# Feed-forward of a float32 block chain on one core: next group's operands made later in a step, early tiles evicted unscaled, sums of the first activations put off to the down product

## What is computed

```python
D_FF = int(math.ceil(8 * D_MODEL / 3 / 256)) * 256      # 2816

def _swiglu(xn, w_gate, w_up, w_down):
    g = jnp.einsum('bsd,df->bsf', xn, w_gate)
    up = jnp.einsum('bsd,df->bsf', xn, w_up)
    return jnp.einsum('bsf,fd->bsd', jax.nn.silu(g) * up, w_down)

        h = _swiglu(_rmsnorm(x, pre_ffn_g[layer]), ffn_w_gate[layer], ffn_w_up[layer], ffn_w_down[layer])
        x = x + _rmsnorm(h, post_ffn_g[layer])
```

## Time and profile before

| what | value |
|---|---|
| median of 3 runs | 4546.69 us (4539.64 to 4556.09) |
| the profiled execution | 4558.02 us |
| its span (first to last instruction) | 4555.0 us |
| PE busy | 4088.6 us (90% of the span) |
| DVE busy | 2750.5 us (60%) |
| ACT, POOL busy | 1402.6 us (31%), 1232.8 us (27%) |
| mean granted TensorE clock | 0.933 of full |
| the two feed-forwards | near 530 to 1220 us and near 1960 to 2650 us |

### The profile page before, as it was taken

One profiled execution on the slowest core, in us unless ns is written; L12 is line 12 of the kernel. 1 busy time (PEld: TensorE's weight loads), 2 busy tenths in 40 slices (PEclk: granted clock), 3 DMA queues, 4 the chain that ended last, 5 costly groups with the idle time before them and its releaser, 6 DMA issues.

```text
span 4555.0 us, 48262 instructions
## 1 busy us (share of the span) xinstructions
PE 4088.6 (90%) x18826; PEld 3185.6 (70%) x18826; DVE 2750.5 (60%) x3035; ACT 1402.6 (31%) x1771; POOL 1232.8 (27%) x586
## 2 busy tenths in 40 slices
PE   7899799989889998889998868998999999899778
PEld 6457677877666666768776657886888888766556
DVE  6744788887754543488887766214665664365543
ACT  4333322233332333232233332222222222155311
POOL 1002144444312322134444421221211111121141
PEclk9999899999899999999999988998999998899788
DMA  2002223343310001222234332222111112221242
GB/s 101 19 14 77 75 97 104 102 140 125 114 56 19 24 19 33 93 81 98 98 120 146 111 116 74 99 96 99 36 56 59 52 59 92 75 94 54 81 145 86
DMA packets 124811, 368.43 MB, mean 81 GB/s; under 512 B 12708, under 2 KB 13352, under 8 KB 118568
## 3 DMA queue, kind: packets, MB, share of 16 engines
q1 hardware_dynamic: 124584, 365.36, 23.4%
HBM read 268.31 MB, written 96.99 MB: 80 GB/s over the span
## 4 chain that ended last, share of the span: by engine, by line
PE 62%; DVE 28%; ACT 3%; DMA 3%; issue 2%; POOL 1%; SPq 0%; DVEq 0%; POOLq 0%; ACTq 0%
PE ps L355 21%; PE ps L1261 13%; PE ps L426 7%; PE ps L772 2%; PE ps L2656 2%; PE ps L2668 2%; DVE h L1430 2%; PE ps L1980 2%; PE ps L2664 2%; PE ps L1972 1%; DVE xop L1421 1%; DVE ua L1560 1%; DVE h L1441 1%; DMA f<-h_keep 1%; PE ps L3706 1%
## 5 line engine op out<-in xcount | busy, mean ns | idle before, releaser
L308 POOL TENSOR_TENSOR wlo<-wraw,whi 128x1024 fp32r<-128x1024 f32 x177 | 429.5, 2427 | 1899.1 <-ACT whi L300 1794.7
L1261 PE MATMUL ps<-xop,whi 128*128 128x512 f32 x1984 | 618.8, 393 | 8.4 <-DVE xop L1421 4.0
L1261 PE MATMUL ps<-top,whi 128*128 128x512 f32 x1488 | 491.2, 413 | 93.3 <-DVE vb L1521 49.3
L300 ACT ACTIVATE whi<-wraw 128x1024 fp32r<-128x1024 f32 x177 | 187.5, 1059 | 1067.0 <-PE ps L355 729.4
L1261 PEld LDWEIGHTS ps<-xop,whi 128*128 128x128 f32 x1984 | 372.8, 188 | 94.9 <-DVE xop L1421 4.8
L1261 PEld LDWEIGHTS ps<-top,whi 128*128 128x128 f32 x1488 | 291.6, 198 | 175.5 <-DVE vb L1521 52.7
L1261 PE MATMUL ps<-xop,wlo 128*128 128x512 f32 x992 | 389.0, 392 | 0.0
L426 PE MATMUL ps<-xhalf,whi 128*128 128x512 f32 x1024 | 378.1, 452 | 5.2 <-POOL wlo L308 5.2
L1610 POOL TENSOR_TENSOR wlo<-wsum,whi 128x1024 fp32r<-128x1024 f32 (+2 forms) x108 | 248.1, 2298 | 470.9 <-ACT whi L1286 470.0
L355 PE MATMUL ps<-xhi,whi 128*128 128x512 f32 x912 | 328.8, 443 | 39.8 <-DVE xlo L561 25.9
L355 PE MATMUL ps<-xhalf,whi 128*128 128x512 f32 x1024 | 280.8, 397 | 27.4 <-DVE xhalf L561 14.4
(11 more groups left out here) (571 smaller groups left out, 7714.0 us busy)
## 6 DMA issues: line engine op xcount, KB each, us to landing
wraw<-in_w_dram SPq DMA_DIRECT2D x177, 512.0 KB, 3.7
h_keep<-h SPq DMA_DIRECT2D x154, 256.0 KB, 4.3
wraw<-in_s_dram SPq DMA_DIRECT2D x48, 512.0 KB, 4.2
f<-h_keep SPq DMA_DIRECT2D x24, 768.0 KB, 5.3
wmore<-in_s_dram SPq DMA_DIRECT2D x32, 512.0 KB, 4.1
x_keep<-x SPq DMA_DIRECT2D x16, 1024.0 KB, 3.9
g_keep<-gates SPq DMA_DIRECT2D x64, 256.0 KB, 2.4
gb<-g_keep SPq DMA_DIRECT2D x32, 512.0 KB, 5.3
```

The lines of the kernel that those rows point to most:

```text
L300: se.own().activation(K.hi(c), K.raw[:, c % NRAW, :], ACT.Copy).then_inc(*K.S(("hi", c)))
L308: ge.own().tensor_tensor(K.lo(c), K.raw[:, c % NRAW, :], K.hi(c).bitcast(F32), SUB).then_inc(*K.G(("lo", c)))
L1261: d = pe.e.matmul(out[:, s, :], w[:, o], x[:, i, :], start=(j < 3 and i == 0 and t == 0), stop=(i == k - 1 and t == 2), skip_group_check=True)
```

## The change

It does five things in each feed-forward.

1. In the lead all four tiles of pair 0 are evicted by ACT as they are (`evict(i, m)`), so the up tiles leave PSUM by ACT and not by DVE's product. DVE scales all four in SBUF after the first operand, and multiplies gate by up later (`early_product`, unit 2 of step 0).
2. The four sums of pair 0 are no longer made in step 0. Its four products are stored as halves (`early_store`), loaded back in unit 3 of step 10 (`early_load`), summed on DVE at the end of step 10, and the sums stored at the beginning of step 11.
3. Pair 0 takes the last place in `h_keep` (`ORDER`), with the weight rows packed to match, so that its sums are needed by the last set only.
4. A set's operands are made later: high parts at j - 3, low parts at j - 4. So ACT makes operands 0 to 3 in the last step of a set and 4 to 6 in the first of the next, DVE 0 to 2 and 3 to 6. Of those, operand 5 and 6 now come after U2 on DVE.
5. ACT's operand 5 of step 0 waits for the four early stores in place of seven stores.

The diff, without the two lines that only rename:

```diff
+ORDER = [*range(1, 11), 0]
...
-        self.early = [at(eb + o * KB, [128, 1024], F32, "h") for o in (-16, -12)]
-        h = self.early
-        self.hq0 = [h[0][:, LOW], h[1][:, LOW], h[1][:, HIGH], h[0][:, HIGH]] + [at(eb + o * KB, [128, 512], F32, "h")[:, :] for o in (-8, -6, -4)]
+        self.early = [[at(eb + o * KB, [128, 1024], F32, "h")[:, :] for o in p] for p in ((-16, -4), (-12, -8))]
+        self.hq0 = [at(xb + (16 + 2 * i) * KB, [128, 512], F32, "h")[:, :] for i in range(7)]
...
 def ffn_lead_scalar(se, K, F):
+    def evict(i, m):
+        se.wait_ge(*K.at("tile", (n, "gate", i), m))
+        se.own().activation(F.early[i][m].rearrange("p (a b) -> p a b", a=2), K.pair((n, "gate", i), m), ACT.Copy).then_inc(*K.S((n, "evicted", i, m), ("free", ((n, "gate", i), m))))
     def settle(se, K):
-        for i in range(2):
-            if i:
-                se.wait_ge(*K.at(N.name, "add", 7))
-            se.wait_ge(*K.at("tile", (n, "gate", i), 0))
-            se.own().activation(F.early[i][:, :].rearrange("p (a b) -> p a b", a=2), K.pair((n, "gate", i), 0), ACT.Copy).then_inc(*K.S((n, "evicted", i), ("free", ((n, "gate", i), 0))))
+        evict(0, 0)
+        evict(0, 1)
+        se.wait_ge(*K.at(N.name, "add", 7))
+        evict(1, 0)
...
-    se.wait_ge(*K.at("tile", (n, "gate", 1), 1))
+    evict(1, 1)
     se.own().activation(F.ohi[2], F.X[:, 0::2, HIGH], ACT.Copy).then_inc(*K.S((n, "ohi", 0, 2)))
     seven_high(se, K, F, 1)
-    se.wait_ge(*K.at(n, "early scaled", 1))
-    se.own().activation(F.early[1][:, :], F.early[1][:, :], ACT.Silu).then_inc(*K.S((n, "early silu", 1)))
+    for i in range(2):
+        se.wait_ge(*K.at(n, "early scaled", i, 0))
+        se.own().activation(F.early[i][0], F.early[i][0], ACT.Silu).then_inc(*K.S((n, "early silu", i)))
...
-            if j >= 2 and next_set(b) is not None:
-                operand_high(se, K, F, next_set(b), j - 2)
-            if j < 2 and b and next_set(b - 1) is not None:
-                operand_high(se, K, F, next_set(b - 1), j + 5)
+            if j >= 3 and next_set(b) is not None:
+                operand_high(se, K, F, next_set(b), j - 3)
+            if j < 3 and b and next_set(b - 1) is not None:
+                operand_high(se, K, F, next_set(b - 1), j + 4)
...
-        if b == NB1:
+        if b in (NB1, NB1 + 1):
             for i in range(7):
-                ve.wait_ge(*K.at(n, "stored", NB1, i))
+                ve.wait_ge(*K.at(n, "stored", NB1 if b == NB1 else 0, i))
...
             if b == 0 and j == 2:
+                early_product(ve, K, F, 0)
+                early_product(ve, K, F, 1)
                 operand_low(ve, K, F, 0, 3)
-                activation_sums(ve, K, F, 0)
...
+            if b == NB1 and j == 6:
+                ve.wait_ge(*K.at(n, "early back"))
+                activation_sums(ve, K, F, 0)
...
-            if j >= 2 and next_set(b) is not None:
-                operand_low(ve, K, F, next_set(b), j - 2)
-            if j < 2 and b and next_set(b - 1) is not None:
-                operand_low(ve, K, F, next_set(b - 1), j + 5)
+            if j >= 4 and next_set(b) is not None:
+                operand_low(ve, K, F, next_set(b), j - 4)
+            if j < 4 and b and next_set(b - 1) is not None:
+                operand_low(ve, K, F, next_set(b - 1), j + 3)
...
+def early_load(sy, K, F):
+    for j in range(7):
+        sy.wait_ge(*K.at(n, "stored", NB1, j))
+    for slot, j in ((0, 0), (3, 2), (1, 4), (2, 6)):
+        sy.e.dma_start(F.hq0[slot], K.keep_h[j][:, place_of(0), :]).then_inc(*K.h_back((n, "early back")))
...
             if j == 2 and b == 0:
-                activation_store(sy, K, F, 0, (0, 1, 2, 3, 4, 5, 6))
+                early_store(sy, K, F)
+            if j == 3 and b == NB1:
+                early_load(sy, K, F)
+            if j == 0 and b == NB1 + 1:
+                activation_store(sy, K, F, 0, (3, 4, 5, 6))
```

More of the change, by code:

```diff
@@ L1363, in ffn_scalar @@
                     se.own().activation(F.ohi[3], F.olo32[3], ACT.Copy).then_inc(*S((n, "ohi", 0, 3)))
-            if j == 4 and b == 0:
-                for i in range(7):
-                    se.wait_ge(*K.at(n, "stored", 0, i))
-                se.wait_ge(*K.at(n, "T", 5))
-                se.own().activation(F.ohi[5], F.X[:, 1::2, LOW], ACT.Copy).then_inc(*S((n, "ohi", 0, 5)))
             c = 7 * b + j + 2
@@ L1371, in ffn_scalar @@
                 seven_high(se, K, F, c)
+            if j == 3 and b == 0:
+                for i in range(4):
+                    se.wait_ge(*K.at(n, "early stored", i))
+                se.wait_ge(*K.at(n, "T", 5))
+                se.own().activation(F.ohi[5], F.X[:, 1::2, LOW], ACT.Copy).then_inc(*S((n, "ohi", 0, 5)))
             if j == 6 and up:
@@ L1487, in ffn_lead_vector @@
     operand_low(ve, K, F, 0, 1, X[:, 1::2, HIGH])
-    early(1)
+    ve.wait_ge(*K.at(N.name, "rs"))
+    for m in range(2):
+        for i in range(2):
+            t = F.early[i][m]
+            ve.wait_ge(*K.at(n, "evicted", i, m))
+            ve.own().tensor_tensor(t, t, N.rs[:, :], MUL).then_inc(*V((n, "early scaled", i, m)))
     operand_low(ve, K, F, 0, 2, X[:, 0::2, HIGH])
```

41 lines of the change are left out of this document (20 added, 21 removed).

## The result

The changed kernel took 4514.0 us (median of 4 runs, 4505.0 to 4522.7), the kernel before beside it 4547.6 (4 runs, 4539.6 to 4556.1): 33.6 us less, ratio 0.9926, 95% interval 0.9899 to 0.9953. It is faster, by a little under half of the 69 us forecast, and at the very edge of the range, beyond its end of 4514 by 0.03 us. Two further groups of runs of the same kernel gave 0.9896 (0.9879 to 0.9912) and 0.9913 (0.9892 to 0.9933), which is 49 and 44 us less; their medians, 4507.0 and 4511.7, lie inside the range.

What follows compares the result with a forecast made beforehand. PE was taken to set the pace, with DVE as what it waits for. Gains of 48.4 (steps 12 to 17), 8 (steps 10 and 11) and 12.6 (lead) sum to 69 us: 4546.7 - 69 = 4477 us, range 4454 to 4514.

Steps and rivals of the forecast that it cites:

- The stall that the prediction named: Down product, step 14: U2 stands on DVE behind operand 6, whose load is late; PE idles 5.51 us before unit 3.
- the signs of being right: Four U2 waits become one of about 6 us; steps 12 to 17 about 178; step 0's unit 5 four to six earlier.
- the signs of being wrong: U3 or operand waits over 3 us in steps 12, 14, 16; step 11 stall over 4; step 0's unit 5 not before 595.
- I leave 1 us for each of the three transitions: Steps 12 to 17: 3 us a layer stay lost between sets, so gains are 22.9 and 25.5, together 48.4 us.
- a slack of 1.4 us: Step 14: U2 would end at 1094.7 or so, where PE would want it at 1096.1.
- plus 2 to 4 where POOL is in the way: Down product: DVE's 5.7 us of work between U2 and U3 grows by 2 to 4 where GpSimd interferes.
- The four sums ... I take 4 ... I take 1 ... 1 us more: Steps 10 and 11: pair 0's sums take 4 us of DVE; 1 us reaches PE, late operand 0 adds 1.
- the sets: Steps 12 to 17 of the down product: a gain of 48.4 us in both layers, bounds 27 to 54.4.
- the gain I named for the schedule there, 6 a layer: Steps 10 and 11: 1.5 at step 10, 3.5 from step 11's U3 wait and 1 from the clock.
- the 1.5 us that I took: Step 10: waits for late operands go, between nothing and 3 of the 7.25 us wait for U2; 1.5 taken.
- The lead: Before and in step 0: a gain of 6.3 us a layer, 12.6 in all; bounds 3 and 10 a layer.
- DVE becomes the bound of the down product: Rival, chance 0.20: stall returns before units 5 or 6, half the sets' gain, nothing in steps 10 and 11; 4507 us.

Runs made afterwards that it cites:

- run 4: The changed kernel with pair 0's sums, their loads and late stores left out, three more products stored early in step 0: 4505.7 us.
- run 1: The changed kernel again, with no edit, for a second profile: 4507.0 us, ratio 0.9896 to the kernel before.
- Run 2: The kernel before with only the later making of operands (part 4) added: 4507.9 us, ratio 0.9898 to the kernel before.
- runs 5 and 7: The changed kernel with operands 4, 5 and 6 one unit later: 4517.3 us; the same with pair 0's sums also moved to step 13: 4509.1 us.

## Why the prediction had the right stall and twice the gain

Of the 69 us forecast, 44.7 came in the feed-forwards, and 33.6 in the median of the recorded runs. The stall that the prediction named is gone, by the mechanism that it named; the terms for what comes after it were too good. Of the signs of being right, one wait for U2 in place of four and 178 us for steps 12 to 17 didn't come (four waits, 12.7 us in all; 185.3 and 185.4 us); the signs of being wrong didn't come either. In the order of their size:

- **"I leave 1 us for each of the three transitions"** is the step that failed most. Steps 14 and 16 take 31.4 to 31.9 us, 2.3 to 2.7 above 29.15, and step 12 without pair 0's sums 31.6, 2.5 above: 7.4 a layer in place of 3, so 8.8 us are missing in both. Of the 7.4, 4.5 are waits for U2 and some 1.6 waits for U3 (in the first layer). Behind it stand two errors. The prediction read a slack of 1.4 us from the row at 1098.49, "after as many operands as it will now have to make". That was a miscount: at 1093.5 DVE had made three since 1084.06 (operands 3, 4 and 5), and in the new order it has to make four ahead of U2 (1 to 4). The fourth takes 1.87 us with its gap, and the slack is gone before GpSimd comes in. The other error is the place of GpSimd's share ("plus 2 to 4 where POOL is in the way"): it was put between U2 and U3 only, and it fell in front of U2 as well. ACT, no longer held up, makes two weights' high parts with one operand between them (1084.81, 1087.35), GpSimd works on both, and operand 4 takes 1.47 us more. In the row of the old order GpSimd was idle until 1099.49.
- **"The four sums ... I take 4 ... I take 1 ... 1 us more"** (2 in all for a layer) is the step that failed worst for its size: they cost 5.9 (run 4 against run 1), and the steps 10 and 11 gain nothing instead of 8. Of that, 1.6 a layer are in step 12, outside the two steps that I had looked at; with these 3.1 us, the 8.8 and step 17's 3.3 the 15 that the sets lack are complete. Run 2 shows that the gain I named for the schedule there, 6 a layer, was nearly right: 5.1 and 4.8. The additions themselves took 4.3 us, as forecast, and found their input there. What I had not costed is what stands behind them: DVE's weight sum, for which SyncE's next load waits, and behind that load the four stores and then all loads of the next set, 5.0 us late. And I had priced each transfer by its median, 4.3 us for a store and 5.3 for an operand. The stores kept it (4.1), but the operands' loads, issued in one bunch with the weights', took 9.7 and 11.0 (into f and into top) where they took 4.7 and 4.5 in run 4.
- **Step 17** stood in no sum. It is the last step, ran free before (29.09), and now takes 30.6 to 30.8: DVE enters it 2.8 us later against PE than before, and the weights of unit 2 come late by 1.3. Another 3.3 us in both layers.
- In **step 10** the wait for U2 stayed at 7.66 where 7.25 was; the 1.5 us that I took came out as nothing, which was my lower bound.
- **The lead** was right in its sum: 11.4 us for 12.6, unit 3 at the old time behind a wait of 7.94 (forecast: about 8), unit 5 at 594.41, which is 592.2 on the clock of the profile before, whose feed-forward began 2.25 us earlier (forecast: 590 to 592). The wait in front of unit 5 was 4.24 and 3.04 us in the two layers, not 2. That DVE and GpSimd follow each other was taken into this sum in full.
- **"DVE becomes the bound of the down product"** (0.20, 4507) was the rival that came nearest, and it is what the rows show. In step 14 DVE has no gap and is busy for 29.7 of 31.4 us. The prediction's test of it, 18.8 + 4 x 1.76 = 25.9 for the first step, has the same miscount: DVE makes six of the seven operands within the first step's window and one in the second's (four and three before), and 18.8 + 6 x 1.76 = 29.4, over the 29.15 that PE takes; from the window of step 14 before it is 27.3 + 2 x 1.76 = 30.8. In the second step's window DVE was busy for 19.48. The stall was said to return in front of units 5 or 6; there it is 0.3 to 0.8 us, and most of it is at U2. That DVE's load as a whole sets the stall is read from its timeline and from runs 5 and 7, whose gains in one step are given back in others; it wasn't tried by taking work away from DVE.
- The part that belongs to no step is the 10 us by which the profiled execution was longer outside the feed-forwards. I had put all of the spread into the mechanisms and none there.
